# A long convolution whose transforms run over even and odd tokens apart, on 128 frequencies

## Chip, core and metric

The kernel runs on one core of a Trainium2 chip. The metric is the device time in microseconds (us); a measurement is the median of several runs. The core has TensorE (matrix products), VectorE, ScalarE and GpSimd (elementwise work), and SyncE, which here issues DMAs. Each engine executes its own list of instructions in order, and semaphores tie the lists together. Products are written to PSUM, eight banks of 128 x 512 float32; everything else lives in SBUF, 128 partitions wide. In rows of the profile these engines are PE, DVE, ACT, POOL and SP, and PEld is TensorE's loading of weights.

## The reference

The reference runs two blocks of a network on 256 tokens and a width of 1024. The change touches only the Hyena part of the second block, a long convolution in both directions of 512 channels, done twice, each time followed by a gate.

```python
def long_conv_bidir(u, h_fwd, h_bwd, bias):          # u: 256 tokens x 512 channels
    k2 = concatenate([h_fwd, zeros((1, C)), h_bwd[:0:-1]], axis=0)
    U = rfft(u, n=2 * L, axis=1)
    K = rfft(k2, n=2 * L, axis=0)
    y = irfft(U * K[None], n=2 * L, axis=1)[:, :L]
    return y + u * bias

def hyena_mixer(...):
    u = short_conv(concatenate([hv, hx1, hx2]), conv_w, conv_b)
    z, gates = u[0], u[1:]
    for n in range(2):
        z = gates[n] * long_conv_bidir(z, filt[:, 0, n], filt[:, 1, n], bias[n])
```

The filters `filt` come from a small network with sines, times a decay over the tokens. Everything is float32. Transforms are taken by the kernel at 256 frequencies that lie symmetrically about the middle of the band, as products with matrices of cosines and sines. Beside Hyena the same stage has eight heads of neighbourhood attention (a softmax over 512 keys) and the projections of the tokens.

## The kernel before

**Weights.** The large products are of float32 weights in three parts. ScalarE copies a tile of 128 x 1024 weights that a DMA brought to `stage` into `wh` (L350), VectorE takes the rest into `wl` (L356: `stage` minus `wh`), and TensorE does for each block of 128 x 128 weights `wh`·`xh`, `wl`·`xh` and `wh`·`xl` (L415 to L417), where `xh` and `xl` are the tokens, split the same way. A tile is eight blocks and 24 matmuls. The split of each tile on VectorE is written four tiles ahead of its use (`lo_part(*four_ahead(...))`). Attention and Hyena use plain float32 matmuls; each of those stands as two records in the trace.

**Start of the kernel.** The small network gives `hid`; TensorE makes the filter taps (L1729: eight products of 128 tokens, weights `hid`, moving side `wboth`, which GpSimd prepares at L732), VectorE multiplies them with the decay (L1159), and TensorE makes the filter spectra (L1738, 16 products over two token halves, and L1741, four more with 65 rows for the extra term), one PSUM bank for each of order, part (real, imaginary) and half of the frequencies. ScalarE copies them to `kre` and `kim` (`spectrum_stored`, L836). On VectorE the taps stand among the pooling steps of the first block (`pool_mixed`; `next_lo`, L1209, is the low part of its next input), and the same ScalarE list makes the high part (L825). Behind the spectra TensorE makes the statistics of the next normalization (L1747).

**Mixer stage.** A loop of `MIXER_TILES` = 28 tiles, n = 0 to 27: 12 tiles of Hyena projection and 16 of gates. The order of each engine is written by hand, as tests on n:
- TensorE (list from L2025 on): the 24 matmuls of the tile; then `na_turn` (L1957, eight transposes of probabilities, n = 4, 7, ... 25), `na_attend` (L1969, n = 5, 8, ... 26) and `na_score` (L1948, n = 2, 5, ... 23) for one attention unit each; `turn_hyena` (L1982) after 5 and 8; `spectrum` (L1997) after 9, 10, 18 and 19, two parts each of two 128x512 products; `inverse_tokens` (L2008) after 13 and 15, four products of 128x512 each; `inverse_channels` (L2022) after 22 to 25, four products of 128x256 each.
- VectorE: for tile n first `na_back` of the unit scored at n - 1 (L1596 and L1598: reciprocal of the sum and scaling `hc`, for which the turn waits), before it or after it by n what follows: `conv_sides` (L1578, L1581), `na_front` (L1589 bias add in PSUM, L1591 maximum), the split L356, `spectrum_product` (L1613, L1614, L1617: real part; at 10, 11, 19, 20), `second_signal` (L1622, at 15), `hyena_out` (L1627, at 23 and 25: the product with the second gate) and `hyena_out_lo` (L1633, at 25 and 27), the low part of the output `yh` for the mix stage that follows.
- ScalarE: copies of tiles out of PSUM, `na_exponentials` (L1036), the turned probabilities back (L1045), Hyena tokens (L1056), `spectrum_back` (L1064: both parts of a spectrum, 128x512 each, from banks 6 and 7 to `ure`/`uim`).
- GpSimd: the imaginary part of the products (L792, L793, L796), three operations for each half, as soon as that half's spectrum is back.

Banks 6 and 7 hold, in turn, the spectra, the inverse to tokens and the inverse to channels. The first convolution goes back to tokens (its result is gated and transformed again), the second to channels.

## Time and profile before

| | |
|---|---|
| time, median of 3 runs | 1047.18 us (1047.04 to 1047.43) |
| the profiled execution | 1046.43 us |
| its span | 1044.7 us |
| TensorE busy | 1004.6 us, 96% of the span |
| VectorE busy | 764.4 us, 73% |
| ScalarE busy | 497.5 us, 48% |
| GpSimd busy | 139.1 us, 13% |
| mean granted clock of TensorE | 0.985 of 2.4 GHz |
| groups L415, L416, L417 of the 256-token weights, idle before them | 11.3, 0.0, 0.0 us |

The busy shares are means over stages of different kinds. What sets the end is read from the chain of waits, which is followed back from the last instruction; how long an engine stood still ahead of an instruction, and for what, stands in brackets at the end of a row of the timeline. TensorE's clock is granted at one of two levels, 1.2 or 2.4 GHz, and a stretch between them has a mean that says how much of it was at which.

### The profile page before, as it was taken

How to read it: one execution, taken by the hardware profiler on the slowest of the kernel's cores; microseconds unless marked ns; L12 is line 12 of the kernel's file. 1: busy time of each engine (PE TensorE's matmuls, PEld its weight loads, DVE VectorE, ACT ScalarE, POOL GpSimd, SP SyncE). 2: the span in 40 equal slices, each digit the busy share in tenths (PEclk: the TensorE clock that was granted, in tenths of full speed). 3: DMA queues.
4: the chain of work that ended last, by engine and by line, in shares of the span. 5: the costliest groups of instructions: out<-in, count | busy, mean ns of one | idle time of the engine just before them, and what ended most of it. 6: DMA issues, size and time to landing. Idle time of an engine off the chain costs nothing.

```text
span 1044.7 us, 20358 instructions
## 1 busy us (share of the span) xinstructions
PE 1004.6 (96%) x7736; PEld 943.4 (90%) x7736; DVE 764.4 (73%) x1223; ACT 497.5 (48%) x728; POOL 139.1 (13%) x153
## 2 busy tenths in 40 slices
PE   5999999999999998999999999999999999999996
PEld 4379999999999988999999998987788999999996
DVE  6669888888866657998867765766455879866554
ACT  6355544444645534454444432564446555554441
POOL 4000000012000036300015400111110330000111
PEclk9699999999999998999999999999999999999998
DMA  7048777667733334566635632442233548644552
GB/s 250 1 161 290 264 271 259 204 240 246 251 123 122 122 104 159 201 240 238 229 127 192 228 127 86 164 145 91 100 123 122 185 176 296 249 163 173 167 178 84
DMA packets 38493, 186.80 MB, mean 179 GB/s; under 512 B 4936, under 2 KB 8809, under 8 KB 25578
## 3 DMA queue, kind: packets, MB, share of 16 engines
q1 hardware_dynamic: 38442, 186.09, 51.2%
q8 instruction: 35, 0.57, 0.2%
q14 instruction: 16, 0.13, 0.0%
HBM read 185.03 MB, written 1.05 MB: 178 GB/s over the span
## 4 chain that ended last, share of the span: by engine, by line
PE 87%; DVE 7%; ACT 2%; issue 2%; POOL 1%; DMA 0%; SPq 0%; DVEq 0%; ACTq 0%
PE ps L415 25%; PE ps L417 25%; PE ps L416 25%; DVE wl L356 2%; PE ps L1729 1%; PE ps L1997 1%; PE ps L1948 1%; PE ps L1738 1%; PE ps L1969 1%; PE ps L1957 1%; PE ps L1773 1%; PE ps L2022 1%; PE ps L2008 1%; DVE xl L1209 1%; ACT wh L350 1%
## 5 line engine op out<-in xcount | busy, mean ns | idle before, releaser
L415 PE MATMUL ps<-xh,wh 128*128 128x256 f32 (+3 forms) x1808 | 525.4, 291 | 11.3 <-DVE xl L1209 3.6
L417 PE MATMUL ps<-xl,wh 128*128 128x256 f32 (+3 forms) x1808 | 518.5, 287 | 0.0
L416 PE MATMUL ps<-xh,wl 128*128 128x256 f32 (+3 forms) x1808 | 517.7, 286 | 0.0
L356 DVE TENSOR_TENSOR wl<-stage,wh 128x1024 fp32r<-128x1024 f32 (+2 forms) x320 | 364.0, 1148 | 133.6 <-ACT wh L350 131.4
L350 ACT ACTIVATE wh<-stage 128x1024 fp32r<-128x1024 f32 (+2 forms) x320 | 306.6, 968 | 181.0 <-PE ps L417 148.3
L415 PEld LDWEIGHTS ps<-xh,wh 128*128 128x128 f32 x1808 | 342.9, 190 | 18.7 <-issue 6.4
L416 PEld LDWEIGHTS ps<-xh,wl 128*128 128x128 f32 x1808 | 342.9, 190 | 3.1 <-issue 1.4
L417 PEld LDWEIGHTS ps<-xl,wh 128*128 128x128 f32 x1808 | 341.4, 189 | 1.4
L415 PE MATMUL ps<-gh,wh 128*128 128x256 f32 (+1 forms) x528 | 150.1, 284 | 2.9 <-DVE wl L356 1.5
L416 PE MATMUL ps<-gh,wl 128*128 128x256 f32 (+1 forms) x528 | 149.4, 283 | 0.0
L417 PE MATMUL ps<-gl,wh 128*128 128x256 f32 (+1 forms) x528 | 148.9, 282 | 0.0
L415 PEld LDWEIGHTS ps<-gh,wh 128*128 128x128 f32 x528 | 99.5, 188 | 3.7 <-DVE gl L1312 2.0
L416 PEld LDWEIGHTS ps<-gh,wl 128*128 128x128 f32 x528 | 99.1, 188 | 0.0
L417 PEld LDWEIGHTS ps<-gl,wh 128*128 128x128 f32 x528 | 99.2, 188 | 0.0
L741 POOL TENSOR_TENSOR norm<-h 128x256 f32 (+1 forms) x31 | 25.3, 817 | 539.5 <-DVE h L1198 303.1
L893 ACT ACTIVATE gh<-up_t 128x256 f32 (+3 forms) x66 | 27.9, 423 | 117.0 <-DVE up_t L1307 77.8
L1254 DVE CUSTOM_DVE_ANT_0 dump<-adaw,cvec 128x1024 bf16<-128x1024 f32 x40 | 49.3, 1233 | 0.3 <-DMA adaw<-in_w_ada 0.3
L888 ACT ACTIVATE gate_t<-gate_t 128x256 f32<-128x256 f32 (+1 forms) x66 | 29.7, 450 | 34.7 <-DVE gate_t L1293 34.5
L1312 DVE TENSOR_TENSOR gl<-up_t,gh 128x256 f32 (+3 forms) x66 | 28.6, 433 | 12.0 <-ACT gh L893 11.4
L1293 DVE TENSOR_TENSOR gate_t<-ps,norm 128x272 f32<-128x272 f32 (+2 forms) x66 | 28.1, 426 | 3.0 <-ACT cvec L900 1.9
L1297 DVE TENSOR_TENSOR up_t<-ps,norm 128x272 f32<-128x272 f32 (+2 forms) x66 | 28.2, 427 | 2.4 <-PE ps L417 2.3
L743 POOL TENSOR_TENSOR norm<-norm 128x256 f32<-128x256 f32 (+1 forms) x31 | 28.3, 914 | 2.4
(247 smaller groups left out, 800.8 us busy)
## 6 DMA issues: line engine op xcount, KB each, us to landing
stage<-in_w_gu SPq DMA_DIRECT2D x66, 1024.0 KB, 4.8
stage<-in_w_dn SPq DMA_DIRECT2D x48, 704.0 KB, 4.1
adaw<-in_w_ada SPq DMA_DIRECT2D x48, 512.0 KB, 5.4
stage<-in_w_gates SPq DMA_DIRECT2D x8, 1024.0 KB, 5.0
stage<-in_w_hy SPq DMA_DIRECT2D x6, 1024.0 KB, 4.8
stage<-in_w_q SPq DMA_DIRECT2D x8, 512.0 KB, 4.8
stage<-in_w_k SPq DMA_DIRECT2D x8, 512.0 KB, 5.2
stage<-in_w_v SPq DMA_DIRECT2D x8, 512.0 KB, 5.2
```

What stands on the lines that cost most here:

```text
L350: nc.scalar.activation(wh[:, b, w], stage[:, b, w], ACT.Copy).then_inc(split_hi, 1)
L356: nc.vector.tensor_tensor(wl[:, b, w], stage[:, b, w], wh[:, b, w].bitcast(fp32), ALU.subtract).then_inc(split_lo, 1)
L415: nc.tensor.matmul(psum, wh[:, b, w], xhi, start=first and n == 0, stop=False)
L416: nc.tensor.matmul(psum, wl[:, b, w], xhi, start=False, stop=False)
L417: last = nc.tensor.matmul(psum, wh[:, b, w], xlo, start=False, stop=close and n == len(blocks) - 1)
L743: pool.tensor_tensor(ssq[:, 0:width], ssq[:, 0:width], sq[:, 0:width], ALU.add)\
L888: act.activation(gate_t[:, b, 0:width], gate_t[:, b, 0:width], ACT.Silu, **({"bias": gate_t[:, b, width:width + 1]} if shifted else {}))\
L893: act.activation(gh[:, ds(m, 1), 0:width], up_t[:, b:b + 1, 0:width], ACT.Copy)\
L1254: ins = dve.tensor_tensor_reduce(out=dump[:, 0, :], in0=adaw[:, b, :], in1=cvec[:, 0, :], scale=1.0, scalar=0.0, op0=ALU.mult, op1=ALU.add ...
L1293: dve.tensor_tensor(gate_t[:, b, 0:w], ps[2 * b][:, 0:w], rstd[:, 0:w], ALU.mult)\
L1297: dve.tensor_tensor(up_t[:, b, 0:w], ps[2 * b + 1][:, 0:w], rstd[:, 0:w], ALU.mult)\
L1312: dve.tensor_tensor(gl[:, ds(m, 1), 0:width], up_t[:, b:b + 1, 0:width], gh[:, ds(m, 1), 0:width].bitcast(fp32), ALU.subtract).then_inc(ac ...
```

## The change

**Transforms.** The 256 frequencies are symmetric about the middle, so frequency f and its mirror share the same products up to the sign that an even or an odd token gives. The tokens are split into even and odd ones. For 128 frequencies the transform of the even tokens and that of the odd ones are made apart, each with one product of 128 rows; the sum of the two is one half of the spectrum, the difference the other. Going back, the sum and the difference of the two halves of the product spectrum are formed first (`product_folded`), and each then gives the tokens of one parity with one product. The cosine and sine matrices shrink to a quarter for the way in (128 x 2 x 128) and to a half for the way back. Columns of one parity are read with a step of two (`t:TX:2`), and `hyena_out` writes them back in the order of the tokens.

**Filter spectra.** Each product makes the transform of one parity alone, ten products where there were twenty; ScalarE stores these halves in `spectra`, and VectorE joins them later, in the q2 tiles ahead of the mixer (`spectrum_halves`, four times two operations). The taps are made by parity. The constants come in seven DMAs where there were five, the decay in two where there was one.

**Mixer.** `spectrum` makes one part of one order at each call (n even: real, n odd: imaginary), at tiles 9, 10, 16 and 17. ScalarE copies one bank only (`second_half_back`), VectorE joins it with the other bank (`spectrum_joined`, sum and difference). Both VectorE's products and GpSimd's imaginary part then wait for `spec_folded`, the joined halves of both parts. VectorE folds the real part at tiles 11 and 18 and GpSimd's imaginary part at 13 and 20. `inverse_tokens` stands at 14, `inverse_channels` at 21 and 22 with eight products of 128 columns each, `hyena_out` at 22 and 23 and its low part at 24 and 25; ScalarE's `hyena_out_hi` at 23 and 24.

The diff, cut to its core (lines of the changed kernel are further down by 6 to 45):

```diff
+SPECTRUM_AT = (9, 10, 16, 17)
...
+def PARITY(part, f):
+
+    return 1 - f if part == 0 else f
...
-        kre = sb("kre", [P, 2, 2, HYW])
-        kim = sb("kim", [P, 2, 2, HYW])
-        cosf = sb("cosf", [P, 2, TX])
-        sinf = sb("sinf", [P, 2, TX])
-        cosi = sb("cosi", [P, 2, TX])
-        sini = sb("sini", [P, 2, TX])
+        spectra = sb("spectra", [P, 4, 2, HYW])
+        kre, kim = spectra[:, 0:2, :, :], spectra[:, 2:4, :, :]
+        cosf = sb("cosf", [P, 2, P])
+        sinf = sb("sinf", [P, 2, P])
+        cosi = sb("cosi", [P, TX])
+        sini = sb("sini", [P, TX])
...
+            pool.wait_ge(k_folded, 4)
             for o in range(2):
+                pool.wait_ge(spec_folded, 2 * o + 2)
                 for f in range(2):
                     n = 2 * o + f
...
-                    pool.wait_ge(spec_re, 2 * (n + 1))
...
-            def spectrum_back(n, part):
-
-                act.wait_ge(spec, 2 * n + part + 1)
+            def second_half_back(n):
+
+                act.wait_ge(spec, 2 * n + 2)
                 if n >= 2:
-                    act.wait_ge(prod_re, n - 1)
-                    act.wait_ge(prod_im, n - 1)
-                act.activation((ure, uim)[part][n % 2], halves(ps[6 + part][:, :]), ACT.Copy).then_inc(spec_re, 1)
+                    act.wait_ge(prod_re, 2)
+                    act.wait_ge(prod_im, 2)
+                act.activation((ure, uim)[n % 2][1], halves(ps[7][:, :]), ACT.Copy).then_inc(spec_second, 1)
...
-                if n in (9, 10, 18, 19):
-                    for part in range(2):
-                        spectrum_back((9, 10, 18, 19).index(n), part)
+                if n in SPECTRUM_AT:
+                    second_half_back(SPECTRUM_AT.index(n))
...
-                if n in (24, 26):
+                if n in (23, 24):
                     for m in range(2):
-                        hyena_out_hi(n - 24 + m)
+                        hyena_out_hi(2 * (n - 23) + m)
...
+            def spectrum_halves(g):
+
+                first, second = (spectra[:, g, f, :] for f in range(2))
+                link(dve.tensor_tensor(first, first, second, ALU.add))
+                dve.scalar_tensor_tensor(out=second, in0=second, scalar=-2.0, in1=first, op0=ALU.mult, op1=ALU.add)\
+                    .then_inc(k_folded, 1)
+            dve.wait_ge(k_read, 8)
             for n in range(4):
                 lo_part(*four_ahead("q2", n))
+                spectrum_halves(n)
...
+            def spectrum_joined(n):
+
+                first, second = (ure, uim)[n % 2]
+                dve.wait_ge(spec_second, n + 1)
+                if n >= 2:
+                    dve.wait_ge(prod_re, 2)
+                    dve.wait_ge(prod_im, 2)
+                link(dve.tensor_tensor(first, halves(ps[6][:, :]), second, ALU.add))
+                dve.tensor_tensor(second, halves(ps[6][:, :]), second, ALU.subtract).then_inc(spec_folded, 1)
...
-                dve.wait_ge(spec_re, 2 * (n + 1))
+                dve.wait_ge(spec_folded, 2 * o + 2)
...
+            def product_folded(o, y, made, folded):
+
+                dve.wait_ge(made, 2 * o + 2)
+                link(dve.tensor_tensor(halves(y[:, 0, :]), halves(y[:, 0, :]), halves(y[:, 1, :]), ALU.add))
+                dve.scalar_tensor_tensor(out=halves(y[:, 1, :]), in0=halves(y[:, 1, :]), scalar=-2.0,
+                                         in1=halves(y[:, 0, :]), op0=ALU.mult, op1=ALU.add).then_inc(folded, 1)
...
-                dve.tensor_tensor(yh[:, m, :], ps[6 + m % 2][:, 0:TX], hyu[:, 8 + m, :], ALU.mult)\
+                by_parity = [a.rearrange("p (j t) -> p t j", t=2) for a in (yh[:, m, :], hyu[:, 8 + m, :])]
+                dve.tensor_tensor(by_parity[0], halves(ps[6 + m % 2][:, 0:TX]), by_parity[1], ALU.mult)\
...
-                if n in (10, 11, 19, 20):
-                    spectrum_product((10, 11, 19, 20).index(n))
+                if n in SPECTRUM_AT:
+                    spectrum_joined(SPECTRUM_AT.index(n))
+                if n in (10, 11, 17, 18):
+                    spectrum_product((10, 11, 17, 18).index(n))
+                if n in (11, 18):
+                    product_folded(n // 18, yre, prod_re, y_re)
+                if n in (13, 20):
+                    product_folded(n // 20, yim, prod_im, y_im)
                 if n == 15:
                     for t in range(2):
                         second_signal(t)
-                if n in (23, 25):
+                if n in (22, 23):
                     for m in range(2):
-                        hyena_out(n - 23 + m)
-                if n in (25, 27):
+                        hyena_out(2 * (n - 22) + m)
+                if n in (24, 25):
                     for m in range(2):
-                        hyena_out_lo(n - 25 + m)
+                        hyena_out_lo(2 * (n - 24) + m)
...
-                pe.matmul(ps[i][:, :], hid[:, 1, t * P:(t + 1) * P], wboth[:, kind, o * HYW:(o + 1) * HYW],
+                pe.matmul(ps[i][:, :], hid[:, 1, t:TX:2], wboth[:, kind, o * HYW:(o + 1) * HYW],
...
-                    ins = pe.matmul(ps[i][:, :], (cosf, sinf)[part][:, t, f * P:(f + 1) * P], gboth[:, o, part, t, :],
-                                    start=t == 0, stop=part == 1 and t == 1)
-                if part == 0:
+                t, shared = PARITY(part, f), part == 0 and f == 0
+                ins = pe.matmul(ps[i][:, :], (cosf, sinf)[part][:, t, :], gboth[:, o, part, t, :], start=True,
+                                stop=not shared)
+                if shared:
...
-                    ins = pe.transpose(ps[6 + t][:, i * P:(i + 1) * P], hyu[:, KN * (j // 2) + i, t * P:(t + 1) * P],
+                    ins = pe.transpose(ps[6 + t][:, i * P:(i + 1) * P], hyu[:, KN * (j // 2) + i, t:TX:2],
...
-            def spectrum(n, part):
-
+            def spectrum(n):
+
+                part = n % 2
                 if n == 0:
-                    pe.wait_ge(hy_tok, 3 + part)
+                    pe.wait_ge(hy_tok, 4)
                 elif n == 2:
                     pe.wait_ge(z1_ready, 2)
                 else:
-                    pe.wait_ge(spec_re, 2 * n + part - 1)
+                    pe.wait_ge(spec_folded, n)
+                for f in range(2):
+                    t = PARITY(part, f)
+                    pe.matmul(ps[6 + f][:, :], (cosf, sinf)[part][:, t, :], ztok[:, t, :], start=True, stop=True)\
+                        .then_inc(spec, 1)
...
+            def inverse_tokens(t):
+
+                pe.wait_ge(spec_folded, 2)
+                pe.wait_ge(y_re, 1)
+                pe.matmul(ps[6 + t][:, :], cosi[:, t:TX:2], yre[:, 1 - t, :], start=True, stop=False)
+                pe.wait_ge(y_im, 1)
+                pe.matmul(ps[6 + t][:, :], sini[:, t:TX:2], yim[:, t, :], start=False, stop=True).then_inc(inv, 1)
+
+            def inverse_channels(m):
+
+                c = slice(m * P, (m + 1) * P)
+                pe.wait_ge(y_re, 2)
+                pe.wait_ge(y_im, 2)
+                if m < 2:
+                    pe.wait_ge(spec_folded, 4)
+                else:
+                    pe.wait_ge(yh_ready, m - 1)
                 for t in range(2):
...
+                    side = ps[6 + m % 2][:, t * P:(t + 1) * P]
+                    pe.matmul(side, yre[:, 1 - t, c], cosi[:, t:TX:2], start=True, stop=False)
+                    ins = pe.matmul(side, yim[:, t, c], sini[:, t:TX:2], start=False, stop=True)
+                ins.then_inc(inv, 1)
...
+                if n == 14:
                     for t in range(2):
-                        inverse_tokens(t, (n - 13) // 2)
-                if n in (22, 23):
+                        inverse_tokens(t)
+                if n in (21, 22):
                     for m in range(2):
-                        inverse_channels(m, n - 22)
-                if n in (24, 25):
-                    for m in range(2, 4):
-                        inverse_channels(m, n - 24)
+                        inverse_channels(2 * (n - 21) + m)
```

The order of the instructions moves with it. VectorE in tile 11 and at the head of tile 12, before: convolution, bias add and maximum of the softmax, split of a tile, the second real product of the first transform, and then the softmax scaling for the turn of tile 13.

```order
L1578 SCALAR_TENSOR_TENSOR hyu<-ps,par,hyu 128x255
L1581 SCALAR_TENSOR_TENSOR hyu<-ps,par,hyu 128x255
L1589 TENSOR_TENSOR ps<-ps,bias 128x2x256
L1591 TENSOR_REDUCE nst<-ps 128x2
L356 TENSOR_TENSOR wl<-stage,wh 128x1024
L1613 TENSOR_TENSOR hyu<-norm,kre 128x512
L1614 TENSOR_TENSOR hyu<-norm,kim 128x512
L1617 TENSOR_TENSOR vxc<-hyu 128x512
L1596 RECIPROCAL nst<-nst 128x2
L1598 TENSOR_SCALAR hc<-hc,nst 128x512 x2
```

The same place in the changed kernel, where L362 is the split, L1643 to L1647 the product, L1652 and L1653 the fold of the real part, L1616 and L1618 the scaling, and `vxc` holds both `yre` and `yim`:

```order
L1598 SCALAR_TENSOR_TENSOR hyu<-ps,par,hyu 128x255
L1601 SCALAR_TENSOR_TENSOR hyu<-ps,par,hyu 128x255
L1609 TENSOR_TENSOR ps<-ps,bias 128x2x256
L1611 TENSOR_REDUCE nst<-ps 128x2
L362 TENSOR_TENSOR wl<-stage,wh 128x1024
L1643 TENSOR_TENSOR hyu<-norm,spectra 128x512
L1644 TENSOR_TENSOR hyu<-norm,spectra 128x512
L1647 TENSOR_TENSOR vxc<-hyu 128x512
L1652 TENSOR_TENSOR vxc<-vxc 128x512
L1653 SCALAR_TENSOR_TENSOR vxc<-vxc 128x512
L1616 RECIPROCAL nst<-nst 128x2
L1618 TENSOR_SCALAR hc<-hc,nst 128x512 x2
```

Between the second product and the scaling two operations of 128x512 have come in. Two places earlier on the same engine (tiles 9 and 10) four more stand ahead of the first product, the joining of the halves.

TensorE at tile 22, before: the last product of the tile, the turn of the softmax probabilities, the first inverse to channels (four products of 256 columns, L2022), the next tile.

```order
L417 MATMUL ps<-xl,wh 128x256
L1957 MATMUL ps<-ident,hc 128x128 x8
L2022 MATMUL ps<-cosi,vxc 128x256
L2022 MATMUL ps<-sini,vxc 128x256
L2022 MATMUL ps<-cosi,vxc 128x256
L2022 MATMUL ps<-sini,vxc 128x256
L415 MATMUL ps<-xh,wh 128x256
```

In the changed kernel, with L2002 the turn and L2064 and L2065 the inverse of two channel blocks (eight products of 128 columns), the second pair of blocks stands there; the first pair stands one tile earlier:

```order
L423 MATMUL ps<-xl,wh 128x256
L2002 MATMUL ps<-ident,hc 128x128 x8
L2064 MATMUL ps<-cosi,vxc 128x128
L2065 MATMUL ps<-sini,vxc 128x128
L2064 MATMUL ps<-cosi,vxc 128x128
L2065 MATMUL ps<-sini,vxc 128x128
L2064 MATMUL ps<-cosi,vxc 128x128
L2065 MATMUL ps<-sini,vxc 128x128
L2064 MATMUL ps<-cosi,vxc 128x128
L2065 MATMUL ps<-sini,vxc 128x128
L421 MATMUL ps<-xh,wh 128x256
```

What followed at tiles 23 to 25 has moved up to this place, and the second pair of blocks now waits for `yh_ready`, the outputs of the first pair, one tile after these were begun. VectorE makes them behind its split in tile 22.

## Rows read from the trace of the kernel before

**Rows 1.** The page, part 4: the chain that ended last, by engine, then by line.

```profile
PE 87%; DVE 7%; ACT 2%; issue 2%; POOL 1%; DMA 0%; SPq 0%; DVEq 0%; ACTq 0%
```

**Rows 2.** Chain of waits, mixer: start us, us, what.

```profile
695.38 3.43 PE ps L1997 x8
...
735.95 0.87 PE ps L1957 x8
...
768.10 1.73 PE ps L2022 x8
```

**Rows 3.** Timeline, TensorE, mixer: start us, us, line, operation, [idle before, releaser].

```profile
717.15 1.09 PE L1957 MATMUL ps<-ident,hc 128*128 128x128 f32 x8 [0.39 <-DVE hc L1598]
...
767.00 1.10 PE L1957 MATMUL ps<-ident,hc 128*128 128x128 f32 x8 [0.82 <-DVE hc L1598]
...
796.63 0.38 PE L415 MATMUL ps<-xh,wh 128*128 128x256 f32 x1 [2.31 <-DVE xl L1633]
```

**Rows 4.** Timeline, VectorE, a split in q2.

```profile
656.57 1.23 DVE L356 TENSOR_TENSOR wl<-stage,wh 128x1024 fp32r<-128x1024 f32 x1 [1.64 <-ACT wh L350]
```

**Rows 5.** Timeline, VectorE and then GpSimd, products of the first transform.

```profile
707.16 1.67 DVE L1617 TENSOR_TENSOR vxc<-hyu 128x512 f32<-128x512 f32 x1
...
715.41 0.69 DVE L1617 TENSOR_TENSOR vxc<-hyu 128x512 f32<-128x512 f32 x1
...
699.52 1.29 POOL L792 TENSOR_TENSOR rope<-hyu,kim 128x512 f32<-128x512 f32 x1 [35.11 <-ACT hyu L1064]
...
706.69 1.60 POOL L792 TENSOR_TENSOR rope<-norm,kim 128x512 f32<-128x512 f32 x1 [3.16 <-ACT norm L1064]
```

**Rows 6.** Timeline, VectorE, tiles 11 and 12.

```profile
709.46 0.48 DVE L1578 SCALAR_TENSOR_TENSOR hyu<-ps,par,hyu 128x255 f32<-128x255 f32 x1 [0.63 <-ACT hyu L1022]
...
710.96 0.70 DVE L1589 TENSOR_TENSOR ps<-ps,bias 128x512 f32<-128x512 f32 x1 [0.50 <-PE ps L1948]
...
712.84 1.22 DVE L356 TENSOR_TENSOR wl<-stage,wh 128x1024 fp32r<-128x1024 f32 x1
...
716.22 0.88 DVE L1598 TENSOR_SCALAR hc<-hc,nst 128x512 f32<-128x512 f32 x2
```

**Rows 7.** Timeline, TensorE, tiles 9 to 12.

```profile
692.27 0.37 PE L415 MATMUL ps<-xh,wh 128*128 128x256 f32 x1
...
695.21 1.88 PE L1997 MATMUL ps<-ztok,cosf 128*128 128x512 f32 x4
...
708.76 1.09 PE L1969 MATMUL ps<-hc,vtok 128*64 128x128 f32 x16
...
710.84 0.38 PE L415 MATMUL ps<-xh,wh 128*128 128x256 f32 x1
```

**Rows 8.** Timeline, VectorE, split of tile 26.

```profile
770.13 1.23 DVE L356 TENSOR_TENSOR wl<-stage,wh 128x1024 fp32r<-128x1024 f32 x1 [2.06 <-ACT wh L350]
```

**Rows 9.** Windows: stretch, us, busy of PE PEld DVE ACT POOL, clock, DMA, GB/s.

```profile
44.00:44.50 0.50, 0.50 (x2) 0.18 (x1) 0.47 (x2) 0.00 (x0) 0.00 (x0) 0.64 0.00 0
399.00:407.00 8.00, 6.20 (x33) 5.97 (x32) 2.15 (x3) 1.79 (x2) 2.17 (x3) 0.57 0.64 243
```

**Rows 10.** Timeline, TensorE, ahead of two low stretches.

```profile
28.02 1.22 PE L1729 MATMUL ps<-wboth,hid 64*128 64x512 f32 x1 [5.77 <-POOL wboth L732]
...
398.79 0.38 PE L415 MATMUL ps<-xh,wh 128*128 128x256 f32 x1 [1.81 <-DVE xl L1209]
...
401.21 0.58 PE L415 MATMUL ps<-xh,wh 128*128 128x256 f32 x1 [1.80 <-DVE xl L1209]
```

**Rows 11.** Chain of waits, start of the kernel.

```profile
8.38 4.83 PE ps L1706 x10
...
42.04 3.08 PE ps L1738 x4
...
61.26 3.93 PE ps L1747 x16
```

**Rows 12.** Timeline, VectorE, start of the kernel.

```profile
53.08 0.50 DVE L1209 SCALAR_TENSOR_TENSOR xl<-h,par,xh 128x272 fp32r<-128x272 f32 x1 [5.12 <-ACT xh L825]
```

60 lines of the change are left out of this document (19 added, 41 removed).

## The prediction

> **What bounds the kernel now.** I read the page first: the chain that ended last, by engine and line [rows 1]. TensorE holds 87% of it, nearly all of that matmuls. So a microsecond taken from TensorE is a microsecond off the time, as long as nothing makes TensorE wait in its place. Then I read the chain inside the mixer (658 to 797 us), where the transforms lie: four matmuls of 128x512 in plain float32 (eight records) hold the chain for 3.43 us, so 0.86 us each, and four of 128x256 for 1.73 us, so 0.43 each [rows 2]. Third, where TensorE waits there today: 0.39 and 0.82 us for the softmax scaling before a turn, 2.31 us at the mix stage for the last low parts of the Hyena output; 3.5 us in all [rows 3]. Last, VectorE between these points, because the change gives VectorE work: it is not idle in passing, it is in line. TensorE's turn of scores is released by an operation that VectorE reaches only after everything that the code puts ahead of it.
>
> **Work removed from TensorE in the mixer.** Spectra: 16 matmuls of 512 columns become 8, minus 6.9 us. Inverse to tokens: 8 become 4, minus 3.4. Inverse to channels: 16 of 256 columns become 16 of 128. No row shows a float32 product of 128 columns with its weights read so; by half of 0.43 it is minus 3.4, and if each kept 0.43 it is nothing. I take 3.4, since a 512-column one costs just twice a 256-column one [rows 2]. Sum 13.7 us. The wait of 2.31 us at the mix stage also goes (outputs and low parts are made two tiles sooner), and the other two are counted anew below: 3.5 us.
>
> **Work added to VectorE.** Two operations to join halves, four times; two to fold a product, four times; two to fold a stored spectrum, four times. All are 128x512, 0.69 us each, some 1.4 a pair [rows 5]. ScalarE loses four copies. The four pairs on the stored spectra stand in q2 tiles, where VectorE waits 1.64 us for a split of a tile [rows 4]: 1.4 fits in, I cost them at nothing (if the cover is gone, 1.4 us each). The others stand in the mixer, in front of operations on which TensorE waits.
>
> **GpSimd blocks VectorE.** This carries the forecast. The product's last step took 0.69 us with GpSimd quiet and 1.67 us when it began 0.47 us after a GpSimd step; that step itself took 1.60 instead of 1.29, having begun under a VectorE operation [rows 5]. Each waits for the other's whole operation, where both read SBUF. The steps that read PSUM do not: the bias add kept 0.70 us [rows 6] beside GpSimd's last step. Before, GpSimd's part of a product starts one tile apart from VectorE's, and there is one such block per transform. Now both wait for the same event, the joined halves of both parts; six GpSimd steps of 1.29 us run in a row against VectorE's products. Taking turns, each block costs VectorE 1.1 to 1.2 us.
>
> The Trainium skill, page "SBUF — State Buffer", section on the two separate sides, says just this: the pair of ports is an exclusive lock between the two engines, the second fully blocks. By that rule the sum is the one below; without it the time is that of rival A.
>
> **The new waits**, by slots from start to start [rows 2, 6, 7]: a tile 2.85 us (24 matmuls; 2.94 where the first one waits for its weights), a turn 0.9, attend and score 2.1 (708.76 to 710.84), bias and maximum 1.9, a split 1.22 less 0.08 of overlap. Tiles are numbered 0 to 27, n is the tile.
> 1. Turn at tile 13. From the first spectrum, at 695.2 as before, TensorE needs 1.7 + 2.85 + 0.9 + 1.7 + 2.85 + 2.1 + 2.85 + 2.85 = 17.8 us and stands at the turn at 713.0. VectorE has the second spectrum's halves joined at 705.7. Then product 2.1 and two blocks 2.4; convolution 0.95; bias and maximum 1.9; split 1.15 and a block 1.1; product 2.1 and a block 1.2; fold 1.4; scaling 1.05: 721.0. Less 0.5, by which the same sum is late on the kernel before: a wait of 7.5 us instead of 0.39.
> 2. Third spectrum, tile 16: needs the second signal 4 us after tile 15, TensorE is there after 3.75. 0.4 us.
> 3. Turn at tile 19. After the fourth spectrum TensorE has two tiles, 5.7 us; VectorE has copy and split 1.5, joining 1.35, product 2.1 with two blocks 2.4, scaling 1.05 with two blocks 2.3: 10.6. Wait 4.8.
> 4. Inverse at tile 21, which needs the imaginary part folded (tile 20 on VectorE). TensorE from the turn: 8.7 us. VectorE: split 1.15 and block 1.1, product 2.1 and block 1.2, fold 1.4, split 1.15, bias and maximum 1.9, split 1.15, low part 0.35, fold 1.4: 12.9. Wait 4.1.
> 5. Inverse at tile 22, channels 256 on: it needs the outputs of the first two, which VectorE makes behind the split of tile 26. Today that split ends 4.3 us after the turn of tile 22 starts [rows 3, 8]; the output adds 0.4; the turn takes 0.9. Wait 3.8, where before one and a half tiles of work lay between.
>
> Together 20.6 us. Mixer without the clock: 20.6 - 13.7 - 3.5 = plus 3.4 us. Queued behind VectorE's late scaling are its splits for tiles 16 and 17, which come in time.
>
> **The clock.** TensorE fell from 2.4 to 1.2 GHz in the idle of 5.77 us before 28.0 us, and again near 399.3 us, amid two waits of 1.81 and 1.80 us with little work between [rows 9, 10]. It came back near 44.3, 2.3 us after full 128-row matmuls began at 42.0. From 399 to 407 us its mean was 0.57: 6.8 us at the low level, so up to 406.1, 4.9 us after work resumed at 401.2. While low, it does half: a fall costs 1.2 to 2.5 us, say 2. Waits of 7.5, 4.8, 4.1 and 3.8 us will bring about three falls, 6 us, of which 2 come back since a slower TensorE waits less for VectorE at the fourth place. Plus 4. Ends: 0 (no fall) and 10 (four of 2.5).
>
> **The start.** Filter spectra: 20 matmuls become 10. The fourth result is ready after 5 instead of 10 matmuls; ScalarE's copy of it is what let the next input and VectorE's last pooling step go at 53.08, after 5.12 us of idle [rows 12]. With five matmuls less at 0.86 (four records in 3.08 us at first, still low [rows 11]) it is due at 48.7, where VectorE is just free: minus 4.4 us up to the statistics matmuls (L1747), which are 8.2 us behind by other work. If the clock, low until 44.3 today, stays low for longer since a 65-row product now follows each first one, only 2.6. But TensorE is then idle for 5 us ahead of L1747: another fall. Its 16 records take 3.93 us; at the low level ten of the same kind took 4.83 [rows 11], so at most 3.8 us are lost, and I take 2. Start: minus 2.4 (ends minus 4.4 and plus 1.2). The loads of constants are halved but in more pieces; they land before VectorE asks, nothing. Columns read with a step of two (weights of 32 matmuls and transposes, moving side of 16) I cost at nothing; no row shows them.
>
> **Sum.** 3.4 + 4 - 2.4 = plus 5.0 us. The profiled execution took 1046.43 us (span 1044.7 and 1.7 around it), 0.75 under the median; against the median of 1047.18 it is 1052.2, so about 1052.
>
> **Rivals.**
> A. The blocks don't occur as I count them (faster). The waits shrink to 3, 0.4, 0.3, 2 and 3.8, 9.5 us: 9.5 - 13.7 - 3.5 = minus 7.7; one fall plus 2; start minus 2.4: minus 8, 1039. For it: only one block per transform was measured, and the order of turns is mine. Against: each overlap on the profile blocks. It decides if VectorE loses under 0.4 us a block. Chance 12%.
> B. The blocks are there but the clock holds at 2.4 GHz in the mixer and at L1747: 3.4 - 4.4 = minus 1, 1046. Against it stand two falls on today's profile, one with waits of 1.8 us. 13%.
> C. The 128-column products and stepped reads are no cheaper than today's: plus 3.4, 1055.5. 10%. The Trainium skill, page "SBUF — State Buffer", says reads stay at full rate with two float32 in a 16-byte line, as a step of two leaves; no run here shows it yet, and by it C is less likely.
> D. The change doesn't do what it says: the matmuls are counted in the order of instructions, so no.
>
> **How the numbers follow.** Forecast 65%: 1052, own range 1047 to 1056. What a measurement of this kernel can tell from no change is 0.2%, 2.1 us: 1045.1 to 1049.3. Slower: the forecast above 1049.3 (53%) and C: 63%. Same: most of B and the low end of the forecast: 19%. Faster: A, a part of B and a start without a fall: 18%. The range takes in B and C and leaves half of A out: 1040 to 1057.
>
> **What would show it.** Right: turns at tiles 13 and 19 that wait 7 and 5 us for VectorE's scaling, inverses at 21 and 22 that wait about 4 each; VectorE's products and splits of 1.7 to 2.4 us beside GpSimd's; clock below 1.0 in the mixer; L1747 starting near 57 us. Wrong: products of 0.69 us throughout, or turns that wait under 3 us.

## The result, and the profile of the changed kernel

The changed kernel takes 1052.03 us (median of 13 runs, 1049.31 to 1053.17), the kernel before 1047.36 us (13 runs, 1044.99 to 1050.45): 1.0041 of it, 95% interval 1.0032 to 1.0051. It is slower by 0.4%, as forecast, and its median is the 1052 of the forecast. The profiled execution took 1051.13 us, with a span of 1049.4 us against 1044.7.

The page, heads of part 1 and part 4 (the chain that ended last, by engine), answering [rows 1]:

```profile
PE 992.7 (95%) x7692; PEld 940.6 (90%) x7692; DVE 788.4 (75%) x1247; ACT 495.0 (47%) x724; POOL 141.5 (13%) x153
...
PE 85%; DVE 8%; ACT 2%; issue 2%; POOL 1%; DMA 0%; SPq 0%; DVEq 0%; ACTq 0%
```

TensorE is busy for 992.7 us where it was 1004.6: the work did go, though part of it ran at the lower clock. The chain holds more of VectorE. Where, the timeline of TensorE in the mixer shows (start us, us, line, operation, idle before and releaser), answering [rows 3]; L2002 is the turn, L2042 a spectrum, L2064 the inverse to channels:

```profile
717.77 1.97 PE L2002 MATMUL ps<-ident,hc 128*128 128x128 f32 x8 [6.77 <-DVE hc L1618]
...
736.83 1.98 PE L2042 MATMUL ps<-ztok,cosf 128*128 128x512 f32 x4 [0.15 <-DVE ztok L1659]
...
755.21 1.97 PE L2002 MATMUL ps<-ident,hc 128*128 128x128 f32 x8 [3.83 <-DVE hc L1618]
...
768.85 0.46 PE L2064 MATMUL ps<-cosi,vxc 128*128 128x128 f32 x2 [1.88 <-issue]
...
778.37 0.76 PE L2064 MATMUL ps<-cosi,vxc 128*128 128x128 f32 x2 [3.75 <-DVE hyu L1665]
```

Five waits at the five places of the forecast: 16.4 us where there were 3.5. (The 1.88 us have no releaser in the row; the last part on which that inverse waits, VectorE's fold L1653, begins at 768.06 and takes 0.69.) Note that the turn takes 1.97 us and not 1.09: the clock is low behind each long wait. VectorE and then GpSimd in tiles 10 and 11 of the same kernel, answering [rows 5] and [rows 6] (L1643 to L1647 the product, L362 the split):

```profile
703.09 0.69 DVE L1643 TENSOR_TENSOR hyu<-hyu,spectra 128x512 f32<-128x512 f32 x1
703.82 1.65 DVE L1644 TENSOR_TENSOR hyu<-hyu,spectra 128x512 f32<-128x512 f32 x1
705.50 1.67 DVE L1647 TENSOR_TENSOR vxc<-hyu 128x512 f32<-128x512 f32 x1
...
708.00 0.69 DVE L1609 TENSOR_TENSOR ps<-ps,bias 128x512 f32<-128x512 f32 x1
...
709.86 2.29 DVE L362 TENSOR_TENSOR wl<-stage,wh 128x1024 fp32r<-128x1024 f32 x1
712.07 1.75 DVE L1643 TENSOR_TENSOR hyu<-norm,spectra 128x512 f32<-128x512 f32 x1
...
709.78 1.29 POOL L806 TENSOR_TENSOR rt<-norm,spectra 128x512 f32<-128x512 f32 x1
711.15 2.13 POOL L809 TENSOR_TENSOR vxc<-rope,rt 128x512 f32<-128x512 f32 x1
```

Four of VectorE's operations take 0.96, 0.98, 1.07 and 1.06 us longer than the same operation alone. The split begins at 709.86, 0.08 us after GpSimd's step at 709.78, and ends at 712.15, after 2.29 us instead of 1.22: it stood for nearly all of GpSimd's step, which was over at 711.07, and then did its own work. GpSimd's next step at 711.15 stands in turn until the split is done. The bias add L1609, which works in PSUM, kept its 0.69 us though GpSimd was at work throughout (from 703.20 to 713.28).

The windows of the changed kernel (stretch, us, busy of PE, PEld, DVE, ACT, POOL, clock, DMA, GB/s) show what the clock did; the second row answers [rows 9]:

```profile
58.00:62.00 4.00, 3.41 (x9) 2.64 (x10) 1.41 (x2) 1.99 (x5) 0.00 (x0) 0.57 0.00 0
399.00:407.00 8.00, 7.06 (x47) 7.01 (x48) 2.26 (x4) 2.02 (x3) 3.06 (x5) 0.79 0.51 197
718.00:724.00 6.00, 6.00 (x31) 6.00 (x31) 3.04 (x4) 1.97 (x2) 0.00 (x0) 0.53 0.02 4
754.00:761.00 7.00, 5.79 (x27) 5.79 (x28) 6.90 (x6) 1.97 (x2) 4.67 (x4) 0.52 0.00 0
778.00:782.00 4.00, 3.63 (x18) 3.66 (x19) 0.56 (x2) 0.00 (x0) 0.00 (x0) 0.57 0.00 0
```

Behind three of the four long waits TensorE works for 6, 5.8 and 3.6 us with a mean of 0.52 to 0.57 of 2.4 GHz, that is, nearly all at 1.2. At that speed these three stretches cost 6.0·0.47 + 5.8·0.48 + 3.6·0.43 = 7.2 us. Behind the wait of 1.88 us the clock stayed at 1.00. And the chain of waits at the start (start us, us, what), answering [rows 11]; L1783 and L1786 are the spectra of the filters, L1792 the statistics:

```profile
41.89 2.00 PE ps L1783 x2
43.90 1.71 PE ps L1786 x2
45.60 3.74 PE ps L1783 x6
49.37 0.60 ACT spectra L849
...
58.59 5.33 PE ps L1792 x16
```

The statistics begin 2.7 us sooner (58.59 for 61.26), but take 5.33 us for 3.93, because the clock fell in an idle time of 4.96 us ahead of them.

**The balance** of the two profiled executions, plus 4.7 us of span: start minus 1.3 (minus 2.7 plus 1.4). The stretch near 400 us minus 1.3: its clock was low for less long, 0.79 over 8 us for 0.57. No term of the forecast has it, and whether the change has a part in it is not shown: of the experiments below some have it as short as here and some as long as before. The mixer plus 7.2: the first attention scores are 2.57 us ahead of the kernel before (663.53 for 666.10), what follows the mixer is 4.67 behind. In it waits plus 12.9, work minus 13.7, and so 8 us for the clock, where the windows above show 7.2.

### The profile page after: what moved, and what is told of

The parts are those of the page before. It is cut to its first block, busy times and chain, and to the rows that moved or that the text cites. A ratio compares the mean times of both kernels' runs of the same rounds, so it can differ in the third digit from the quotient of the medians.

```text
span 1049.4 us, 20288 instructions
## 1 busy us (share of the span) xinstructions
PE 992.7 (95%) x7692; PEld 940.6 (90%) x7692; DVE 788.4 (75%) x1247; ACT 495.0 (47%) x724; POOL 141.5 (13%) x153
## 4 chain that ended last, share of the span: by engine, by line
PE 85%; DVE 8%; ACT 2%; issue 2%; POOL 1%; DMA 0%; SPq 0%; DVEq 0%; ACTq 0%
PE ps L421 25%; PE ps L423 25%; PE ps L422 25%; DVE wl L362 2%; PE ps L1774 1%; ACT wh L356 1%; PE ps L2002 1%; PE ps L1993 1%; PE ps L1818 1%; PE ps L2014 1%; DVE xl L1221 1%; PE ps L1783 1%; PE ps L1836 1%; PE ps L1792 1%; POOL wboth L744 0%
## 5 line engine op out<-in xcount | busy, mean ns | idle before, releaser
L362 DVE TENSOR_TENSOR wl<-stage,wh 128x1024 fp32r<-128x1024 f32 (+2 forms) x320 | 366.6, 1156 | 121.5 <-ACT wh L356 120.0
L753 POOL TENSOR_TENSOR norm<-h 128x256 f32 (+1 forms) x31 | 24.6, 792 | 549.6 <-DVE h L1210 303.1
```

Source lines behind the costliest of these rows:

```text
L362: nc.vector.tensor_tensor(wl[:, b, w], stage[:, b, w], wh[:, b, w].bitcast(fp32), ALU.subtract).then_inc(split_lo, 1)
```

## The experiments

All are of the changed kernel, if nothing else is said. Two questions are at stake: why VectorE is late, and what the clock adds.

**GpSimd's products left out.**

```diff
-                    link(pool.tensor_tensor(ut3, ure[f], halves(kim[:, o, f, :]), ALU.mult))
-                    link(pool.tensor_tensor(ut4, uim[f], halves(kre[:, o, f, :]), ALU.mult))
...
-                    pool.tensor_tensor(halves(yim[:, f, :]), ut3, ut4, ALU.add).then_inc(prod_im, 1)
+                    pool.memset(yim[:, f, 0:8], 0.0).then_inc(prod_im, 1)
```

> The changed kernel with GpSimd's three operations for each imaginary product left out (a memset of 8 columns signals in their place); the imaginary half of the inverse then reads leftovers. TensorE and VectorE keep every instruction. Theory (VectorE is late because it and GpSimd exclude each other): VectorE's L1644, L1647, the split after them and the first operation of the next product fall from 1.65, 1.67, 2.29 and 1.75 us to 0.69, 0.69, 1.22 and 0.69, the turn at tile 13 waits 6.77 - 4.1 = 2.7 us, the turn at tile 19 under 0.5 instead of 3.83; 7.4 us less waiting, and one or both low-clock stretches behind them gone, 3 us each: 1038 to 1042. Rival 1 (the added joins and folds alone make VectorE late): both waits stay within 1 us of 6.8 and 3.8, time 1049 to 1052. Rival 2 (the waits fall but the clock is low all the same): 1044 to 1045.

Measured: 1042.64 us (1042.26 to 1044.88), 0.9962 of the kernel before (0.9945 to 0.9979). VectorE's product and split, and the turn at tile 13 (lines here are 2 lower), from the timelines of this run:

```profile
704.96 0.69 DVE L1642 TENSOR_TENSOR hyu<-hyu,spectra 128x512 f32<-128x512 f32 x1
705.68 0.69 DVE L1645 TENSOR_TENSOR vxc<-hyu 128x512 f32<-128x512 f32 x1
...
709.07 1.22 DVE L362 TENSOR_TENSOR wl<-stage,wh 128x1024 fp32r<-128x1024 f32 x1
710.20 0.69 DVE L1641 TENSOR_TENSOR hyu<-norm,spectra 128x512 f32<-128x512 f32 x1
...
714.84 1.97 PE L2000 MATMUL ps<-ident,hc 128*128 128x128 f32 x8 [2.70 <-DVE hc L1616]
```

VectorE's and TensorE's lists are unchanged, and the waits are 2.70 and under 0.3 us, as the theory said to the tenth; rival 1 is out. The time is 0.6 us above the range, since waits of 2.70, 1.87 and 3.74 us remain and the turn still takes 1.97 us: the clock falls behind 2.70 us as well. Behind the turn at 19, which no longer waits, it held; so rival 2, by which the clock is low all the same, came true at one of the two turns.

**GpSimd started later.** The same question without leaving work out.

```diff
             for o in range(2):
-                pool.wait_ge(spec_folded, 2 * o + 2)
+                pool.wait_ge(na_prob, 2 * o + 4)
```

> The changed kernel with one wait of GpSimd moved: its imaginary products start only after the softmax scaling of unit 3 (the turn of tile 13) or unit 5 (tile 19), not as soon as the halves are joined; all else is unchanged and the result complete. Theory (VectorE loses a GpSimd step each time it meets one): VectorE's products and the split between them take 0.69 and 1.22 us again, the turn at 13 waits 2.7 us and that at 19 under 0.5, as without any imaginary product; but GpSimd's six steps now end 8 to 10 us later, so the imaginary fold and the inverse behind it are late: about 4.9 us of wait at tile 14 and 8 us at tile 21, 1051 to 1055 in all. Rival (VectorE's steps are long for another reason than GpSimd's running beside them): they stay at 1.65 to 2.3 us and the turn at 13 waits 6.8.

Measured: 1055.84 us (1053.83 to 1057.08), 1.0073 of before (1.0053 to 1.0093). From the timelines, VectorE and then TensorE:

```profile
706.14 0.69 DVE L1644 TENSOR_TENSOR hyu<-hyu,spectra 128x512 f32<-128x512 f32 x1
...
710.25 1.22 DVE L362 TENSOR_TENSOR wl<-stage,wh 128x1024 fp32r<-128x1024 f32 x1
...
726.02 0.69 DVE L1652 TENSOR_TENSOR vxc<-vxc 128x512 f32<-128x512 f32 x1 [5.22 <-POOL vxc L809]
...
716.02 1.51 PE L2002 MATMUL ps<-ident,hc 128*128 128x128 f32 x8 [2.70 <-DVE hc L1618]
...
727.49 2.08 PE L2051 MATMUL ps<-vxc,sini 128*128 128x512 f32 x2 [2.83 <-DVE vxc L1653]
...
771.21 0.77 PE L2064 MATMUL ps<-cosi,vxc 128*128 128x128 f32 x2 [7.49 <-issue]
```

The result is complete, VectorE's steps are short again, and the turn waits the same 2.70 us. So it is when GpSimd runs, not how much VectorE has to do, that made 4.1 of the 6.8 us. But the price is only moved, and the time is 0.8 us above the expected range: GpSimd starts at the scaling's end (716.11) and not at 703, VectorE stands for 5.22 us at the fold, the inverse at tile 14 waits 2.83 us (4.9 were expected) and that at tile 21 waits 7.49 (8 expected). A lone change of GpSimd's start doesn't pay.

**VectorE's second product behind the scaling.**

```diff
-                if n in (10, 11, 17, 18):
-                    spectrum_product((10, 11, 17, 18).index(n))
-                if n in (11, 18):
+                if n in (10, 12, 17, 18):
+                    spectrum_product((10, 12, 17, 18).index(n))
+                if n in (12, 18):
```

> The changed kernel with VectorE's second product and the fold of the real part moved from tile 11 to tile 12, behind the softmax scaling; no instruction more or less. Theory (the turn at tile 13 waits for what stands ahead of the scaling in VectorE's list): product 2.1 plus a block 1.06 and fold 1.4, 4.5 us, leave the path of the scaling; the split's block stays and the scaling may catch one of 1.1: the turn waits 2.3 to 3.9 us instead of 6.77, the inverse at tile 14 waits up to 0.8, time 3 to 4 us lower, and up to 3 more if the clock then holds: 1045 to 1049. Rival (the turn waits for the exponentials on ScalarE or for the maximum, not for the product): the wait stays above 6 us and the time at 1052.

Measured: 1047.98 us (1046.08 to 1052.12), 1.0011 of before (0.9996 to 1.0027).

```profile
714.91 1.88 PE L2002 MATMUL ps<-ident,hc 128*128 128x128 f32 x8 [3.00 <-DVE hc L1618]
```

3.8 us less at this turn, 4.1 in the median. Nothing was added or taken away: the wait is a matter of what stands ahead of the scaling in one engine's list. The three other waits stayed as they were (3.89, 2.04 and 3.74 us). The scaling itself took 1.70 us instead of 0.88 here, being beside GpSimd's last step.

**The two pairs of the inverse to channels further apart.**

```diff
-                if n in (21, 22):
+                if n in (21, 23):
                     for m in range(2):
```

> The changed kernel with the second pair of the inverse to channels one tile later (21 and 23 instead of 21 and 22; outputs 22 and 24, high parts 23 and 25, low parts 24 and 26). Theory (VectorE makes the first outputs only behind the split of tile 26, for which ScalarE waits on TensorE, and TensorE stands ahead of the second pair): the wait of 3.75 us at tile 22 goes to 0, and with it the low clock of 3.4 us behind it, 1.7 us: 1046 to 1048.5. Rival (the wait moves to the mix stage, for the low parts of the outputs, as 2.3 us in the kernel before): 1050 to 1052.

Measured: 1045.47 us (1044.51 to 1047.45), 0.9981 of before (0.9969 to 0.9994): 6.6 us less, a microsecond more than the theory allowed. The second pair doesn't wait (its first row has no bracket), and runs at the full clock, 0.39 us for two records instead of 0.63 to 0.76 (rows of the timeline overlap; from start to start two records are 0.23 us):

```profile
778.15 0.49 PE L2064 MATMUL ps<-cosi,vxc 128*128 128x128 f32 x2
778.49 0.39 PE L2065 MATMUL ps<-sini,vxc 128*128 128x128 f32 x2
```

The mix stage did not wait in its place. To move this one pair by one tile turns the loss into a gain of 0.2%. The microsecond over is at least in part the clock: behind the turn at 19 it was low for some 3.5 us in this execution and for 6 in the changed kernel's.

**Waits filled with matmuls that nobody uses.**

```diff
+            pe.wait_ge(k_read, 1)
+            for i in range(5):
+                pe.matmul(ps[0][:, :], cosf[:, 0, :], gboth[:, 1, 0, 0, :], start=True, stop=True)
             pe.wait_ge(k_read, 5)
...
+                if n in (13, 19):
+                    pe.wait_ge(spec_folded, 2 + n // 19 * 2)
+                    for i in range((7, 4)[n // 19]):
+                        pe.matmul(ps[7][:, :], cosf[:, 0, :], ztok[:, 0, :], start=True, stop=True)
```

> The changed kernel with matmuls that compute nothing used, put where TensorE stands idle: five of 128x512 ahead of the statistics L1792, seven ahead of the turn at tile 13, four ahead of the turn at tile 19 (0.86 us each at 2.4 GHz, so 4.3, 6.0 and 3.4 us in idle times of 4.96, 6.77 and 3.83). All waits for VectorE stay as they are. Theory (the low clock follows idle time and costs 1.4 us at the start, 3.0 after tile 13, 3.0 after tile 19): L1792 takes 3.9 instead of 5.3 us, no stretch of low clock in tiles 13 to 20, 5.4 to 7.4 us saved, of which up to 2 come back as a longer wait ahead of the inverse at tile 21 (1.88 today): 1045 to 1048. Rival (the clock falls for another reason, or the low stretches lie where TensorE would wait anyway): 1051 to 1053, the low stretches remain.

Measured: 1049.80 us (1046.17 to 1051.04), 1.0019 of before (1.0005 to 1.0033). Neither said it. Statistics, the turn at 19 and the inverse at 21, then three windows of this run:

```profile
58.77 3.94 PE L1795 MATMUL ps<-squares,ones 128*128 128x272 f32 x16 [0.67 <-ACT spectra L849]
...
751.99 1.09 PE L2005 MATMUL ps<-ident,hc 128*128 128x128 f32 x8 [0.42 <-DVE hc L1618]
...
764.64 0.57 PE L2067 MATMUL ps<-cosi,vxc 128*128 128x128 f32 x2 [3.60 <-issue]
...
754.00:761.00 7.00, 7.00 (x65) 6.16 (x63) 6.83 (x9) 2.69 (x5) 1.60 (x2) 1.00 0.06 8
764.00:769.00 5.00, 4.36 (x24) 4.39 (x25) 2.64 (x5) 0.45 (x1) 0.00 (x0) 0.66 0.36 104
775.00:782.00 7.00, 6.23 (x29) 6.26 (x30) 0.95 (x3) 0.00 (x0) 0.00 (x0) 0.51 0.01 2
```

Where the idle time was filled the clock stayed up (3.94 us of statistics, a turn of 1.09, a clock of 1.00 where it was 0.52). That part of the theory holds. But TensorE then reached tile 21 early and waited 3.60 us there instead of 1.88, and the clock fell behind that wait and the next. In the profiled executions TensorE stood at tile 21 5.9 us sooner than in the changed kernel (at 761.04 for 766.97). Of these 1.7 went into the longer wait, 1.6 into the low clock behind it, 1.2 into the longer low clock behind the next wait, and it ended 1.4 us ahead; in the medians 2.2 us were left of the 7.4. A microsecond given to TensorE ahead of a wait for VectorE is handed back in good part behind it.

**The filter spectra issued twice**, so that the start has twenty products again.

```diff
-                ins = pe.matmul(ps[i][:, :], (cosf, sinf)[part][:, t, :], gboth[:, o, part, t, :], start=True,
-                                stop=not shared)
+                for again in range(2):
+                    ins = pe.matmul(ps[i][:, :], (cosf, sinf)[part][:, t, :], gboth[:, o, part, t, :], start=True,
+                                    stop=not shared)
```

> The changed kernel with each of the ten products of the filter spectra issued twice, the second time with the same result, so that TensorE has twenty of them as in the kernel before; the mixer is untouched. Theory (the halved filter stage is worth 2.7 us up to the statistics, of which 1.4 are lost again by their low clock after 5 us of idle): L1792 (here some lines lower) starts at 61 to 63 us instead of 58.6 and takes 3.9 us instead of 5.3, time 1 to 2.5 us above the changed kernel: 1053 to 1054.5. Rival (the start is covered by the loads or by VectorE's pooling): no difference, 1052.

Measured: 1053.99 us (1053.27 to 1055.55), 1.0062 of before (1.0048 to 1.0077); the statistics start at 62.21 us, after an idle time of 0.67 instead of 4.96, and are at the full clock. So the halved filter stage is worth 2.0 us, and the rest of the change costs 6.3 (1053.99 against 1047.67 for the kernel before in the same comparison). Most of that is the mixer; 0.95 us stand at the start, where the statistics came at 61.26 before.

**All operations kept, the tiles chosen anew.** If order is the whole loss, an order must undo it.

```diff
-SPECTRUM_AT = (9, 10, 16, 17)
+SPECTRUM_AT = (9, 10, 17, 18)
...
-                if n in (10, 11, 17, 18):
-                    spectrum_product((10, 11, 17, 18).index(n))
-                if n in (11, 18):
-                    product_folded(n // 18, yre, prod_re, y_re)
-                if n in (13, 20):
-                    product_folded(n // 20, yim, prod_im, y_im)
+                for k, at in enumerate((12, 12, 20, 21)):
+                    if n == at:
+                        spectrum_product(k)
+                if n in (12, 21):
+                    product_folded(n // 21, yre, prod_re, y_re)
+                if n in (12, 21):
+                    product_folded(n // 21, yim, prod_im, y_im)
...
-                if n in (21, 22):
+                if n in (23, 25):
```

> The changed kernel with every operation of the new transforms kept and only their tiles moved: spectra at 9, 10, 17, 18; VectorE's products at 12, 12, 20, 21, so that those of the first convolution stand behind the softmax scaling for the turn of tile 13; folds of both parts at 12 and 21; inverse to tokens at 15, second signal at 16; inverse to channels at 23 and 25, outputs and their high parts at 24 and 26, low parts at 25 and 27. Theory (16.4 us of waits and the low clock behind them are the whole loss, and both come from the order): turn at 13 waits at most 1 us, turns at 16 and 19 nothing, turn at 22 1.7, inverse at 23 0.2, the mix stage 2.7 for the low parts, 5.6 us in all; 10.8 us less than 16.4 and most of the 7.6 us of low clock in the mixer gone: 1034 to 1038, clearly below the kernel before. Rival (the work of the joins and folds itself overloads VectorE and GpSimd wherever it stands; the waits only move): 1045 to 1051.

Measured: 1034.06 us (1032.54 to 1035.80), 0.9874 of before (0.9854 to 0.9894). The only waits of TensorE over 0.3 us in the mixer, and windows behind the turns at 13 and 22:

```profile
756.79 1.09 PE L2003 MATMUL ps<-ident,hc 128*128 128x128 f32 x8 [1.29 <-DVE hc L1618]
...
783.20 0.39 PE L421 MATMUL ps<-xh,wh 128*128 128x256 f32 x1 [2.31 <-DVE xl L1671]
...
718.00:724.00 6.00, 6.00 (x43) 4.52 (x40) 5.83 (x9) 0.89 (x2) 0.00 (x0) 1.00 0.00 0
756.00:763.00 7.00, 6.21 (x58) 5.51 (x59) 6.83 (x11) 3.30 (x4) 0.31 (x1) 1.00 0.39 150
```

3.6 us of waits for 16.4, no low clock in the mixer (from 660 to 810 us its mean was 1.00, where the changed kernel has 0.93), 18 us less than the changed kernel and 13.6 less than the one before (1047.67 beside it), with every join, fold and product still there. The blocks became fewer as well. All of VectorE's operations in the mixer that take over 0.3 us longer than alone lose 10.0 us together in the changed kernel, 3.5 in this one and 2.0 in the kernel before: GpSimd's first three steps, of 1.28 us, now run beside VectorE's work on PSUM for the convolution and the softmax. Those that are left (the split at 713.16 takes 2.29 us) stand where nobody waits. How much of the gain is due to fewer blocks and how much to their places is not parted here.

**The same, with the start filled**: the five matmuls ahead of the statistics from above, and nothing else.

> The kernel with the moved tiles, and five matmuls without use ahead of the statistics, 4.3 us in the idle time of 5 us. Theory (the low clock at the statistics follows that idle time): they take 3.9 instead of 5.3 to 6.8 us, 1.4 to 2.8 us less than the kernel with moved tiles alone: 1032 to 1036. Rival (executions differ more in where the clock falls elsewhere than this is worth): within 1 us of the kernel with moved tiles alone.

Measured: 1032.45 us (1029.46 to 1033.05), 0.9847 of before (0.9830 to 0.9865), 1.6 us less than without them; the statistics take 3.94 us instead of 6.99. The intervals of the two ratios overlap, so the size is not settled by the times alone, and that it pays here because no long wait for VectorE stands behind it is argued, not shown. The profiled execution was the slowest of the five, at 1033.05: its taps began at 29.86 us, 2.1 later than without the five matmuls (27.76).

**And the last low parts ahead of the split in tile 27.**

```diff
+                if n == 27:
+                    for m in range(2, 4):
+                        hyena_out_lo(m)
                 lo_part(*four_ahead("hy", n))
```

> The kernel with moved tiles and the busy start, and in tile 27 the two last low parts of the Hyena output ahead of VectorE's split instead of behind it. Theory (the 2.31 us at the mix stage, in the kernel before as in the one with moved tiles, are VectorE waiting for a split whose high part ScalarE makes only after tile 27, while the low parts could have been made since the high parts of the output): the wait goes to 0 and nothing else comes late, 2.3 us less than the kernel with the busy start: 1029.5 to 1031.5. Rival (the next tiles' split is late instead): the same 1032.5.

Measured: 1028.37 us (1026.47 to 1033.55), 0.9826 of before (0.9802 to 0.9850). VectorE makes the low parts at 775.35 and the split at 777.05, and TensorE no longer waits at the mix stage; 1.25 us at tile 22 are its only wait over 0.3 us in the mixer. The median fell by 4.1 us, more than the 2.3 of the wait; the executions of the two overlap. A fall of the clock can be the rest: in the profiled execution with the busy start it fell behind this very wait, to means of 0.86, 0.50 and 0.79 in three windows of 2 us from 781.80 on, 1.7 us lost, and wait and clock make 4.0. It did not fall there in the kernel before, nor in the one with moved tiles alone, so how many of the executions did so is not shown. (The two profiled ones lie 6.4 us apart; the other 2.6 are the taps, which begin at 27.25 here and at 29.86 there.) The 2.31 us of [rows 3] come from the place of these low parts, in the kernel before as well.

```profile
775.35 0.76 DVE L1671 TENSOR_TENSOR xl<-hyu,xh 128x256 fp32r<-128x256 f32 x2 [0.15 <-ACT xh L1082]
777.05 1.23 DVE L362 TENSOR_TENSOR wl<-stage,wh 128x1024 fp32r<-128x1024 f32 x1 [0.95 <-ACT wh L356]
```

**And the idle time ahead of the filter taps filled.**

```diff
+            pe.wait_ge(pool_read, 1)
+            for i in range(24):
+                pe.matmul(ps[0][:, 0:P], ones[:, :], ones[:, :], start=True, stop=True)
             pe.wait_ge(wboth_set, 2)
```

> The same, and 24 matmuls of 128x128 without use (0.23 us each, 5.4 in all) in the idle time of 5.8 us ahead of the filter taps L1774. Open question: the longest low clock of the kernel, from 27.4 to 47.9 us, follows that idle time, but the taps behind it have only 64 rows and the clock did not come back during 14 us of them. Theory 1 (the fall is due to the idle time alone): the taps run at 2.4 GHz, 16 records in 7 to 9 us instead of 14.0, time 4 to 8 us lower, 1022 to 1027. Theory 2 (a stretch of 64-row products does not hold the clock): it falls all the same, one stretch later, and 0 to 2 us are gained: 1028 to 1031.

Measured: 1024.82 us (1023.27 to 1029.01), 0.9794 of before (0.9773 to 0.9815). From the timeline and the windows:

```profile
21.66 5.52 PE L1775 MATMUL ps<-ones 128*128 128x128 f32 x48
27.62 7.14 PE L1781 MATMUL ps<-wboth,hid 64*128 64x512 f32 x16 [0.44 <-POOL wboth L744]
...
27.40:44.20 16.80, 16.58 (x38) 7.20 (x39) 16.11 (x27) 7.30 (x17) 0.16 (x1) 1.00 0.00 1
```

In the profiled execution the taps take 7.14 us instead of 14.02. The median fell by 3.6 us, into the range of theory 1 though short of its gain: VectorE's pooling becomes the bound of the start (VectorE is busy for 16.11 of 16.80 us), and other executions had a lower mean clock. The profiled one, with a mean clock of 0.992, was the fastest of the five; another, at 0.984, took 1029.01.

**Ten instead of five at the statistics.**

```diff
             pe.wait_ge(k_read, 1)
-            for i in range(5):
+            for i in range(10):
```

> The kernel with the busy taps, with ten instead of five matmuls without use ahead of the statistics: 8.6 us in what is now an idle time of 8.5 (the spectra end 5 us earlier than before and the statistics cannot). Theory (the low clock at the statistics followed the 4.05 us that five left idle): L1802 takes 3.9 instead of 5.6 us, and the time falls by 1.7 us to about 1023. Rival: within 0.5 us of 1024.8, because the clock then falls at another of the executions' weak places.

Measured: 1026.45 us (1021.30 to 1032.09), 0.9806 of before (0.9775 to 0.9837). In the profiled execution, at 1021.48, the statistics took 3.85 us and the whole start was at the full clock. But six executions fall into two groups: 1021.3, 1021.5 and 1023.6 with mean clocks of 0.995 and 0.996, and 1029.3, 1030.0 and 1032.1 with 0.987 to 0.989. Against the five at 1023 to 1029 nothing is decided.

**The kernel before, with the 24 matmuls ahead of its taps.**

```diff
+            pe.wait_ge(pool_read, 1)
+            for i in range(24):
+                pe.matmul(ps[0][:, 0:P], ones[:, :], ones[:, :], start=True, stop=True)
```

> The kernel before the change, with the same 24 matmuls without use ahead of its filter taps and nothing else. Theory (the low clock of the taps has nothing to do with the change; the kernel before loses as much by it): its taps take 7 instead of 14.0 us and its spectra start near 35 instead of 42 us, but VectorE's pooling, which ran beside them, now holds part of it: 3 to 7 us faster, 1040.5 to 1044.5. Rival (twenty products behind the taps cover what the taps gain, or the clock falls there all the same): 1046 to 1047.5.

Measured: 1040.03 us (1035.38 to 1049.99), 0.9949 of the kernel before (0.9926 to 0.9972). By the medians (1047.88 before) that is 7.9 us less, by the ratio 5.3; the executions fall into two groups, so that a middle says little. The start of the profiled execution:

```profile
27.45 7.13 PE ps L1732 x16
...
52.63 3.93 PE ps L1750 x16
```

The kernel before pays for the low clock of the start as well, and of the 23 us between 1047.4 and 1024.8 us 5 to 8 could have been had without the change. Of twelve executions nine took 1035 to 1042 us (clock 0.992 to 0.995) and three 1047 to 1050 (0.987). The fill keeps the clock up in most executions, not in all; no profile caught one of the others.

## Why the prediction was right, point by point

**The bound, and the work removed.** TensorE's chain was the right thing to read. Products of 128 columns, for which no row stood, cost 0.23 us (two records), half of 0.43 as taken, with columns read by a step of two (chain of waits, inverse at tile 21):

```profile
769.54 0.23 PE ps L2064 x2
769.77 0.23 PE ps L2065 x2
```

The taps, with stepped weights, took 14.02 us before and after at the low clock, and 7.14 us at the full one, for 7.13 in the kernel before without steps. So rival C is out. The rule of the Trainium skill, page "SBUF — State Buffer", section "Specifications (TRN2)", that two float32 in a 16-byte line keep the full rate, agrees with 0.23 us here.

**GpSimd against VectorE.** The step that carried the forecast was right and is shown, not argued: the same lists give turns that wait 6.77 us, or 2.70 with GpSimd out of the way, by two different edits. By the rule of the Trainium skill, page "SBUF — State Buffer", section on the two separate sides, the second of two such operations stands for the whole of the first; the trace agrees, with a split that began 0.08 us into a step of 1.29 us and lost 1.07. Rival A, in which the blocks fail, was priced too low at 1039 us, if the kernel without GpSimd's products stands for it: that one took 1042.6, since its waits still bring the clock down.

**The five waits**, forecast and measured: 7.5 and 6.77; 0.4 and 0.15; 4.8 and 3.83; 4.1 and 1.88; 3.8 and 3.75; together 20.6 and 16.4. The places, the order and the releasers were right. The blocks were as many as forecast, four ahead of each of the two turns, but too high: I put each at 1.1 to 1.2 us, and they were 0.96 to 1.07 ahead of the turn at 13, 4.1 us together and not 4.7. Ahead of the turn at 19 (two on the product, two on the scaling, which took 2.70 us instead of 0.88) they made 3.8 us and not 4.7. What is left at tile 13, 2.8 us by the forecast, was measured as 2.70 with GpSimd out of the way. The wait at tile 21 was shorter because a TensorE at half clock comes later, as the kernel with filled waits shows (3.60 us where the clock had held). I had booked these 2 us under the clock.

**The clock.** Three falls were forecast and three came, behind the waits I named. The term was mis-sized: a fall behind a wait of 6.8 or 3.8 us cost 2.8 us and not 2, and the 2 us that come back were measured in the waits. Waits and clock together were forecast at 20.6 + 4 = 24.6 us, and measured at 16.4 + 8 = 24.4. So the 1052 was hit by two sizes that were wrong in opposite directions: 4.2 us too much for waits, 4 too little for the clock. Half of each is the 2 us booked under the other name; the rest is luck. The sum of mixer terms, plus 7.4 forecast and 7.2 measured, is better than its parts deserve.

**The start.** Minus 2.4 was forecast, minus 1.3 measured. I took 4.4 us up to the statistics, at five products of 0.86 us; it was 2.7, since the clock stayed low until 47.9 instead of 44.3 us. That was the alternative which I named (2.6) and set aside. The idle time of 5 us and the fall at the statistics came as forecast (1.4 us for 2), and the kernel with the doubled products puts the start at 2.0 us. By the profiled executions mixer and start make plus 5.9, and only the 1.3 us of the stretch near 400 us, which I had not in the sum, bring that to the plus 4.7 of the spans. That is luck too, as far as the profiled executions stand for the others.

**Rival B** (the clock holds) is out by the windows; the changed kernel with filled waits shows that a clock held in two of the three places brings little (2.2 us), because of the waits that follow. What I did not see is that the whole of the loss, and more, lay in the order (1052.0 us in one, 1034.1 in the other): I counted the waits as properties of the change, and they belonged to the tiles that were chosen for it.
